# The expert stage with jobs of 96 tokens in plain float32 on strips of 32 columns, and weights in 8 KB rows

## The reference

```
logits = hf @ w_router + b_router;  top_v, top_e = lax.top_k(logits, 4);  top_w = softmax(top_v)
# the tokens of each expert, padded to blocks of EXPERT_BLOCK = 128 rows
def expert_block(args):
    xb, e = args
    gu = xb @ w_gate_up[e] + b_gate_up[e]                 # [.., 1024] @ [1024, 2048]
    gate = minimum(gu[:, 0::2], 7.0);  up = clip(gu[:, 1::2], -7.0, 7.0)
    act = (up + 1.0) * gate * sigmoid(1.702 * gate)
    return act @ w_down[e] + b_down[e]                    # [.., 1024] @ [1024, 1024]
out = zeros((T, D)).at[row_tok].add(ys * row_w)           # then x = x + gate2 * out
```

## Time and profile before

| | us |
|---|---|
| runs | 1861.49, 1865.33, 4311.42 |
| median | 1865.33 |
| the profiled execution's own time | 1871.22 |
| its span in the trace | 1869.4 |
| mean granted TensorE clock | 0.968 of full |

### The profile page before, as it was taken

The page is one execution under the profiler, slowest core; times in us unless marked ns, Lnnn a source line. Parts: engine busy times, 40 slices in busy tenths (PEclk is TensorE's granted clock), DMA queues, the critical chain, the costliest instruction groups (busy, mean ns, idle before and its releaser), DMA issues.

```text
span 1869.4 us, 30546 instructions
## 1 busy us (share of the span) xinstructions
PE 1771.5 (95%) x10966; PEld 1374.6 (74%) x10966; DVE 1442.8 (77%) x1690; ACT 1102.8 (59%) x1165; POOL 366.0 (20%) x252
## 2 busy tenths in 40 slices
PE   6999997799999869999999999999999999999996
PEld 3444894465588758888888888888888888888884
DVE  3779335653234569999999999999999989989998
ACT  3142331554123227777777777777777777777773
POOL 4000610001000212122122122212213212312321
PEclk9999998799999959999999999999999999999997
DMA  9940000401322179999999999999999999999996
GB/s 334 344 163 1 4 4 3 164 1 46 135 91 91 37 267 353 369 366 371 368 365 372 365 368 369 363 367 365 366 366 368 366 367 365 373 361 366 367 365 235
DMA packets 251970, 500.40 MB, mean 268 GB/s; under 512 B 17243, under 2 KB 19352, under 8 KB 251717
## 3 DMA queue, kind: packets, MB, share of 16 engines
q1 hardware_dynamic: 239814, 481.41, 71.2%
q0 software_dynamic: 9648, 17.33, 3.7%
q10 hardware_dynamic: 2448, 0.78, 0.2%
HBM read 491.06 MB, written 26.23 MB: 277 GB/s over the span
## 4 chain that ended last, share of the span: by engine, by line
PE 62%; DVE 1%; issue 0%; ACT 0%; ACTq 0%; DVEq 0%
PE bank L2051 19%; PE bank L2049 19%; PE bank L2050 19%; PE bank L2046 2%; PE bank L2064 2%; PE bank L2036 1%; DVE sb_mod L2328 0%; DVE sb_x L2331 0%; DVE sb_mod L2335 0%; DVE sb_e_lo L2241 0%; PE bank L2121 0%; ACT sb_e_hi L2127 0%; DVE sb_x L2337 0%; ACT sb_y L2137 0%; ACTq L1988 0%
## 5 line engine op out<-in xcount | busy, mean ns | idle before, releaser
L2241 DVE TENSOR_TENSOR sb_e_lo<-sb_w_raw,sb_e_hi 128x2048 fp32r<-128x2048 f32 x388 | 875.6, 2284 | 1.7 <-ACT sb_e_hi L2127 1.7
L2127 ACT CAST sb_e_hi<-sb_w_raw 128x2048 fp32r<-128x2048 f32 x389 | 743.2, 1911 | 114.1 <-DMA sb_w_raw<-in_w_down_dram 45.6
L2049 PE MATMUL bank<-sb_e_hi,sb_x_hi 128*128 128x512 f32 x1032 | 409.2, 396 | 0.0
L2051 PE MATMUL bank<-sb_e_hi,sb_x_lo 128*128 128x512 f32 x1032 | 405.2, 393 | 0.0
L2050 PE MATMUL bank<-sb_e_lo,sb_x_hi 128*128 128x512 f32 x1032 | 404.2, 392 | 0.0
L2212 POOL TENSOR_TENSOR sb_tick<-sb_ones 128x1 f32<-128x1 f32 x64 | 148.7, 2323 | 855.0 <-DVE sb_row L2311 687.8
L2051 PEld LDWEIGHTS bank<-sb_e_hi,sb_x_lo 128*128 128x128 f32 x1032 | 194.3, 188 | 42.0
L2050 PEld LDWEIGHTS bank<-sb_e_lo,sb_x_hi 128*128 128x128 f32 x1032 | 194.6, 189 | 40.7
L2049 PEld LDWEIGHTS bank<-sb_e_hi,sb_x_hi 128*128 128x128 f32 x1032 | 194.8, 189 | 37.2
L2049 PE MATMUL bank<-sb_e_hi,sb_a_hi 128*128 128x512 f32 x512 | 206.1, 402 | 0.0
L2051 PE MATMUL bank<-sb_e_hi,sb_a_lo 128*128 128x512 f32 x512 | 200.7, 392 | 0.0
(11 more groups left out here) (447 smaller groups left out, 2398.9 us busy)
## 6 DMA issues: line engine op xcount, KB each, us to landing
sb_w_raw<-in_w_gate_up_dram SPq DMA_DIRECT2D x262, 1024.0 KB, 10.0
sb_w_raw<-in_w_down_dram SPq DMA_DIRECT2D x128, 1024.0 KB, 11.4
sb_ring<-in_w_in_dram SPq DMA_DIRECT2D x7, 2048.0 KB, 10.6
sb_x<-in_ada_w_dram SPq DMA_DIRECT2D x8, 1024.0 KB, 9.3
sb_mod<-in_ada_w_dram SPq DMA_DIRECT2D x8, 1024.0 KB, 9.5
sb_ring<-in_ada_w_dram SPq DMA_DIRECT2D x3, 2048.0 KB, 13.9
sb_x<-in_x_dram SPq DMA_DIRECT2D x2, 2048.0 KB, 13.1
sb_ring<-in_w_out_dram SPq DMA_DIRECT2D x2, 2048.0 KB, 7.9
```

The lines of the kernel that those rows point to most:

```text
L2049: te.matmul(out, hi[:, k0 + k, :], w_hi, start=(first and k == 0 and what >= 2 * GU), stop=False)
L2051: mm = te.matmul(out, lo[:, k0 + k, :], w_hi, start=False, stop=(last and k == 3))
L2127: return sc.copy(g.e_hi[:, p % PARTS, :, :], raw(p))
L2241: return ve.tensor_tensor(g.e_lo[:, p % PARTS, :, :], raw(p), g.e_hi[:, p % PARTS, :, :].bitcast(F32), ALU.subtract).then_inc(split_done[p ...
```

## The change

The routing makes jobs of at most CAP = 96 tokens, so that with these inputs there are again 32; a job may also be of an expert without tokens, since each expert now has at least one. The first job is always expert 0's, whose eight pieces of gate and up SP loads at the start of the routing, before h2 is stored and y is set to zero; four pieces of the second job follow once the table is there.

The rounding and its rest are gone: weights, tokens and activations stay float32, and neither ACT nor DVE touches the weights. TensorE's product is made of matmuls whose stationary operand is 128 x 32. The array's four strips of 32 columns work side by side: strips 0 to 2 hold the job's three groups of 32 tokens and take the same 512 columns of gate and up; the fourth strip holds each of the three token groups in turn and takes the last 512 of the 2048 columns (`up`, L2069 and L2070). So three groups of four matmuls do for one k what 2048 columns need. `down` does the same with 256 columns (L2080 and L2081). The results lie in three banks: partitions 0 to 95 of bank r hold column quarter r of all tokens, partitions 96 to 127 hold the last quarter of 32 tokens.

The weights are loaded as [128, 2048] in rows of 8 KB: eight pieces of gate and up, one for each k, and four of down with two k side by side. The ring has 12 places, each used once a turn, and SP waits for TensorE's use of a place alone. A turn of the loop is: the activations turned (6 transposes), three bias matmuls, the next job's gate and up, the features of the job after (8 transposes), this job's down. The first job's gate and up go ahead of the loop, the last one's activations and down behind it; three of the eight matmuls with the down biases come before this last down.

```diff
+G, CAP, STRIP = 3, 96, 32
+SLOTS, UP, DOWN = 12, 8, 4
+SPARE = SLOTS - UP
+BLOCKS = SEQ // CAP + 1
+
+
+def load_up(g, sp, s, e, k):
+
+    src = g.a["w_gate_up"][0][e, P * k:P * k + P, :]
+    sp.dma_start(g.w_raw[:, s, :], src.rearrange("a p n -> p (a n)")).then_inc(g.raw_in[s], 16)
+
+
+def load_down(g, sp, s, e, q, sem):
+
+    src = g.a["w_down"][0][e, 2 * P * q:2 * P * q + 2 * P, :]
+    sp.dma_start(g.w_raw[:, s, :], src.rearrange("a (p r) n -> p (a r n)", r=2)).then_inc(sem, 16)
...
+            for k in ks:
+                load_up(g, sp, k, slice(0, 1), k)
...
+            second = sp.value_load(g.table[0:1, 2:3], min_val=0, max_val=N_EXP - 1)
+            for k in range(SPARE):
+                load_up(g, sp, UP + k, bass.ds(second, 1), k)
...
+            then(ve.tensor_scalar(block_sum, counts, float(CAP), 1.0, ALU.is_gt, ALU.add), "b0")
+            for i in range(1, BLOCKS - 1):
+                then(ve.scalar_tensor_tensor(block_sum, counts, float(CAP * (i + 1)), block_sum, ALU.is_gt, ALU.add), f"b{i}")
...
+            in_expert = ps[1][:, 0:N_EXP * NT].rearrange("p (t e) -> p t e", t=NT)
+            then(ve.tensor_scalar(part, in_expert, 1.0 / CAP, 0.5 / CAP - 0.5, ALU.mult, ALU.add), "part")
+            then(ve.tensor_scalar(whole, part, ROUND, ROUND, ALU.add, ALU.subtract), "whole")
+            then(ve.scalar_tensor_tensor(part, whole, float(P - CAP), in_expert, ALU.mult, ALU.add), "spread")
...
-        pair = ([P, KD, P], F32R)
-        (g.e_hi, g.e_lo, g.x_hi, g.x_lo, g.a_hi, g.a_lo, g.row, g.tick, g.bias_pick) = g.sb(ctx, e_hi=([P, PARTS, 4, 512], F32R), e_lo=([P, PARTS, 4, 512], F32R), x_hi=pair, x_lo=pair, a_hi=pair, a_lo=pair,
-             row=([P, 1], I32), tick=([P, 2], F32), bias_pick=([P, P], F32R))
+        (g.xT, g.aT, g.row, g.tick, g.bias_pick) = g.sb(ctx, xT=([P, KD, CAP], F32), aT=([P, KD, CAP], F32), row=([P, 1], I32), tick=([P, 2], F32),
+             bias_pick=([P, P], F32R))
...
+        def up_slot(k):
+
+            return UP + k if k < SPARE else k - SPARE
+
+        def down_slot(q):
+            return SPARE + q
+
+        def loaded(s, turn):
+
+            return raw_in[s], 16 * turn + (16 if s >= UP else 32)
+
+        def was_used(s, turn):
+
+            return used[s], (turn if s >= UP else turn + 1)
...
+            def rest_of_turn(turn, e, after):
+                for k in range(SPARE, UP):
+                    sp.wait_ge(*was_used(up_slot(k), turn))
+                    load_up(g, sp, up_slot(k), bass.ds(after, 1), k)
+                for q in range(DOWN):
+                    sp.wait_ge(*was_used(down_slot(q), turn))
+                    load_down(g, sp, down_slot(q), bass.ds(e, 1), q, raw_in[down_slot(q)])
+
+            last = last_job(sp)
+            rest_of_turn(0, sp.value_load(g.table[0:1, 1:2], min_val=0, max_val=N_EXP - 1), sp.value_load(g.table[0:1, 2:3], min_val=0, max_val=N_EXP - 1))
+            with sp.Fori(1, last) as turn:
+                e, after = expert(turn), expert(turn + 1)
+                for k in range(SPARE):
+                    sp.wait_ge(*was_used(up_slot(k), turn))
+                    load_up(g, sp, up_slot(k), bass.ds(after, 1), k)
+                rest_of_turn(turn, e, after)
+            e = expert(last)
+            for q in range(DOWN):
+                sp.wait_ge(*was_used(UP + q, last))
+                load_down(g, sp, UP + q, bass.ds(e, 1), q, last_in[q])
...
-            def product(p, what, out, hi, lo):
-
-                if what < 2 * GU:
-                    k0, first, last = 4 * (what % 2), what % 2 == 0, what % 2 == 1
-                else:
-                    k0, first, last = 4 * ((what - 8) // 2), what < 10, what >= 10
-                if first and what < 2 * GU:
-                    te.matmul(out, g.bias_pick[:, :], g.bias[:, 256 * what:256 * what + 512], start=True, stop=False)
-                for k in range(4):
-                    w_hi, w_lo = g.e_hi[:, p % PARTS, k, :], g.e_lo[:, p % PARTS, k, :]
-                    te.matmul(out, hi[:, k0 + k, :], w_hi, start=(first and k == 0 and what >= 2 * GU), stop=False)
-                    te.matmul(out, hi[:, k0 + k, :], w_lo, start=False, stop=False)
-                    mm = te.matmul(out, lo[:, k0 + k, :], w_hi, start=False, stop=(last and k == 3))
+            def bias_rows():
+
+                for b in range(G):
+                    mm = te.matmul(up_bank[b][:, :], g.bias_pick[:, :], g.bias[:, b, :], start=True, stop=False)
                 return mm
 
-            def gate_up(p, turn):
-                te.wait_ge(*is_split(p, turn))
-                product(p, CHUNK_AT[p], ps[CHUNK_AT[p] // 2][:, :], g.x_hi, g.x_lo).then_inc(*pe(f"w{p}"))
-
-            def down(p, turn):
...
-            jobs = job_count(te)
-            te.matmul(ps[5][:, :], g.wT[:, 0:P], g.b_down[:, 0:512], start=True, stop=True).then_inc(*first_pe("y"))
...
+            def up(s, k):
+
+                last = k == UP - 1
+                for r in range(G):
+                    for c in range(G):
+                        at = slice(STRIP * c, STRIP * c + STRIP)
+                        te.matmul(up_bank[r][at, :], g.xT[:, k, at], g.w_raw[:, s, 512 * r:512 * r + 512], start=False, stop=last)
+                    mm = te.matmul(up_bank[r][CAP:P, :], g.xT[:, k, STRIP * r:STRIP * r + STRIP], g.w_raw[:, s, 512 * G:2048], start=False, stop=last)
+                return mm
+
+            def down(s, q):
+
+                for r in range(2):
+                    first, last, k = q == 0 and r == 0, q == DOWN - 1 and r == 1, 2 * q + r
+                    for j in range(G):
+                        for c in range(G):
+                            at = slice(STRIP * c, STRIP * c + STRIP)
+                            te.matmul(down_bank[j][at, 0:256], g.aT[:, k, at], g.w_raw[:, s, 1024 * r + 256 * j:1024 * r + 256 * j + 256], start=first, stop=last)
+                        mm = te.matmul(down_bank[j][CAP:P, 0:256], g.aT[:, k, STRIP * j:STRIP * j + STRIP], g.w_raw[:, s, 1024 * r + 256 * G:1024 * r + 1024],
+                                       start=first, stop=last)
+                return mm
+
+            def activations_turned(turn, marks):
+                te.wait_ge(*vec.before("ac1", turn))
+                te.wait_ge(*act.before("xh", turn))
+                for b in range(G):
+                    if b == 2:
+                        te.wait_ge(*vec.before("ac2", turn))
+                        te.wait_ge(*vec.before("xl", turn))
+                    for r in range(2):
+                        mm = te.transpose(turned(b, r), act_out[:, b, P * r:P * r + P], g.ident[:, :])
+                    if b >= 1:
+                        mm.then_inc(*marks(f"tr{b - 1}"))
+
...
+            for k in range(UP):
+                te.wait_ge(raw_in[k], 16)
+                up(k, k).then_inc(used[k], 1)
+            te.wait_ge(x_in, 32)
+            features(0).then_inc(*first_pe("xt2"))
+            features(1).then_inc(*pe.credit())
+            with te.Fori(0, last) as turn:
+
+                activations_turned(turn, pe)
+                te.wait_ge(*vec.before("bp", turn))
+                bias_rows().then_inc(*pe("bias"))
+                for k in range(UP):
+                    te.wait_ge(*loaded(up_slot(k), turn))
+                    up(up_slot(k), k).then_inc(used[up_slot(k)], 1)
+                te.wait_ge(x_in, 16 * turn + 48)
+                te.wait_ge(*act.at("aT", turn))
+                te.wait_ge(*vec.at("aT", turn))
+                for i in range(2):
+                    features(i).then_inc(*pe(f"xt{i}"))
+                te.wait_ge(*act.before("y", turn))
+                te.wait_ge(*vec.before("y", turn))
+                for q in range(DOWN):
+                    te.wait_ge(*loaded(down_slot(q), turn))
+                    down(down_slot(q), q).then_inc(used[down_slot(q)], 1)
+            activations_turned(last, last_pe)
...
+                mm = down(UP + q, q)
+            mm.then_inc(*last_pe("d"))
...
-            def split(p):
-                return ve.tensor_tensor(g.e_lo[:, p % PARTS, :, :], raw(p), g.e_hi[:, p % PARTS, :, :].bitcast(F32), ALU.subtract).then_inc(split_done[p % PARTS], 1)
```

More of the change, by code:

```diff
@@ L1684, in phase_route @@
         placed = rows[:, 1536:2048].rearrange("p (t k e) -> p t k e", t=NT, k=TOP_K)
-        mask = rows[:, 2048:2304].rearrange("p (t a e) -> p t a e", t=NT, a=2)
+        mask = rows[:, 4096:4608].rearrange("p (t a e) -> p t a e", t=NT, a=4)
+        whole, part = (rows[:, 2048 + 128 * i:2176 + 128 * i].rearrange("p (t e) -> p t e", t=NT) for i in range(2))
         weight = rows[:, 2304:2432].rearrange("p (t e) -> p t e", t=NT)
@@ L2116, in _ @@
-            te.wait_ge(*vec.before("ac0", jobs))
-            te.wait_ge(*act.before("y0", jobs))
-            te.wait_ge(*last_act.at("y1"))
-            for t in ts:
-                for n in range(2):
```

(60 more changed lines are left out.)

496 lines of the change are left out of this document (179 added, 317 removed).

## The result

The changed kernel takes 1796.14 us (median of 4 runs, 1793.59 to 1800.63) against 1863.41 us of the kernel before measured beside it (4 runs, one of them of 4311.42 us, which the median leaves aside): a ratio of 0.965, 95% interval 0.9617 to 0.9683. Timed again in another set it was 0.964 (0.9614 to 0.9665). The forecast was 1808 us, in a range of 1782 to 1848.

What follows compares the result with a forecast made beforehand. TensorE was taken to bound the expert stage. Turns of 33.9 us for 35.65, with start and last down, gave 56.4 us less, the end 1.0: 1871.2 - 57.4 = 1813.8 profiled, median 1808 us, range 1782 to 1848.

Steps and rivals of the forecast that it cites:

- TensorE bounds the stage before: Expert stage of the kernel before: TensorE busy 35.65 of 35.65 us a turn at full clock, DVE 8% behind.
- keep pace by order and are not what is late: Weight transfers before: SP's queue spends 736.9 of 1,000 us waiting for the split, so transfers were not taken as late.
- Four strips at once: Gate, up and down: four full-height operands move together, 0.86 us a group of four; one after another 3.43 us.
- The milder form of the rival: Strips overlapping in part: groups take 1.26 times as long, 8.1 us more a turn, kernel 2066 us; chance 0.03.
- The turn: One turn of the expert loop on TensorE: 33.9 us against 35.65, with 33.0 and 35.2 as ends.
- the changes between strips and the whole array: Four switches a turn on TensorE, 0.15 us each, 0.6 together; ends 0 and 0.4 each.
- The transfers: Weight loads in 8 KB rows: over 400 GB/s, so 32.5 us a turn or less, hidden beside TensorE.
- The rival's bound of 365 at 8 KB: Transfers become the bound: at 365 GB/s the last piece lands at 1800, 15 us more, 1823 us; chance 0.10.
- Rows of 8 KB: Weight loads: longer rows lift transfers from 365 to over 400 GB/s, where the turn would need 384.
- The start: Routing to loop: routing 1 us longer, first activations 3.5 us exposed, loop starting at 722.8 us (before 702.9).
- The end: After the last down: 1.0 us off the 25.7 us before, from between 0 and 4.
- The waits in each turn: Rival: TensorE idle 1 to 2 us a turn around its transposes, 31 to 62 us, 1839 to 1870; chance 0.08.

## Why the prediction was right, step by step

- **TensorE bounds the stage before**: right, 8 KB rows alone changed nothing. But it was half of it. That the transfers "keep pace by order and are not what is late" was true and hid that they had no room. SP's waits for places don't show room: in the changed kernel SP waits 230.6 of 300 us with transfers within 1% of their limit. The DMA share of 1.04 doesn't show the opposite either, with 0.98 where the same kernel could move 7% more. Only the runs with less work for TensorE told. (In the earlier trace rows it is 24 slices, not 26, in which clock and DMA share both stand at nine tenths; nothing hangs on it.)
- **Four strips at once**: right, 4.0 of 4. The milder form of the rival is out: the Trainium skill ("TensorE: Matmul & The Clock Gate", "Measured speedup vs the span model") has three strips at 2.38 times one; here three and four strips in long runs lose nothing, 0.858 us a group like one strip alone.
- **The turn**, 33.9: measured 33.54. The transposes took 1.6 us for 1.7. Of the changes between strips and the whole array, put at 0.6, the chain shows about 0.3, as longer first pieces of down (0.35 for 0.21) and of gate and up (0.56 for 0.42). The range's ends of 33.0 and 35.2 held it; the ends that were named for the changes make only 33.3 and 34.9, and the rest has no source.
- **The transfers**: the mis-sized step. I took "over 400" for 8 KB rows and 32.5 us or less; they do 392 and 33.49. The windows I read it from the earlier trace rows were 4 to 6 us long and had no gathers or adds among them; with few of these the rate is 416. That the answer came out right all the same, by 0.05 us a turn, is luck. Had strips brought a turn to 31 us, the forecast would have been wrong by 2.5 us a turn. The rival's bound of 365 at 8 KB was too low. So, for this program on one core, is the about 358 GB/s per core that the Trainium skill ("DMA: Bandwidth & Descriptors", "Where 436 GB/s comes from") gives as the HBM side's limit: the runs held 392 and 416 over 300 us.
- **Rows of 8 KB** were costed as what hides the transfers; that was needed and right, and worth 2.2 points of the 3.6 once TensorE's turn was short.
- **The start**: routing 1 us longer as forecast (40.41 us from the earlier trace rows's last row to the first features; now 41.38). TensorE's wait for the first activations was 3.06 us for 3.5. Not foreseen: the clock fell again after it, to 718.2, about 2 us.
- **The end**: 2.0 us less for the 1.0 taken.
- **The waits in each turn**: none, TensorE is busy 300.00 of 300 us.

The sum was 17.1 us too long on the span. 7.4 of these are the phases ahead of routing, which were that much shorter in this execution than in the one I summed against, which is chance; 9.3 the loop, 1.6 the start, 1.0 the end, against 2.2 that the last down took longer.

## What to carry to other kernels

Narrow stationary operands pay only when all strips of the array hold work at once and neighbours in the program are on different strips; count strips filled, not matmuls. Neither a wait of the load queue for free places nor the DMA share beside it shows whether transfers have room: ask by a kernel with less for the compute engine to do, and see whether the load queue still waits. Where two bounds stand within a few per cent, a change has to move both, and an experiment on either alone will say that it is worth little. A deep ring hides a shortage for as long as its lead lasts, so read a turn from late in the loop.

## What the runs showed of the hardware

- Sustained weights beside gathers and adds: 366 GB/s with 2 KB rows, 392 with 8 KB; 416 with 8 KB when POOL's queue moves a twelfth of its rows. The DMA share was 1.04, 1.01 and 1.01, and 0.98 in a kernel that asked for only 366 GB/s with 8 KB rows.
- Strips of 32 columns in float32, 128 rows and 512 columns: three or four side by side take 0.858 us a group, 4 records starting within 0.02 us.
- Three matmuls in a row on each strip: 1.47 times the time of the strip work, where nothing overlapping but neighbours would have made 3.3.
- The granted clock fell after 3.06 us without work at 710.7 and not after 1.27 us, in one trace of a kernel with that wait; in the last down it was 0.88 in one trace and 1.00 in another of the same code.
